# The RWKV-7 scan of a streaming encoder: the key turn split by heads and moved to another PSUM bank, key products with 128 stationary columns, and a new order on four engines

## The reference

```python
def step(s, inp):
    r_t, w_t, k_t, v_t, aa_t, bb_t = inp
    sa = jnp.einsum('bhij,bhj->bhi', s, aa_t)
    s = s * w_t[:, :, None, :] + sa[..., None] * bb_t[:, :, None, :] + v_t[..., None] * k_t[:, :, None, :]
    return s, jnp.einsum('bhij,bhj->bhi', s, r_t)

s_last, ys = lax.scan(step, s0.astype(f32),
                      (tm(r_h), tm(w_h), tm(k_h), tm(v_h), tm(-kk), tm(kk * a_h)))
mean = jnp.mean(y, axis=-1, keepdims=True)
var = jnp.mean(jnp.square(y - mean), axis=-1, keepdims=True)
```

## Time and profile before

| | |
|---|---|
| median of 3 runs | 3098.05 us (3096.76 to 3098.19) |
| the profiled execution's own time | 3098.73 us |
| its span | 3096.9 us |
| PE busy in the span | 2966.1 us, 96% |
| DVE, ACT, POOL busy | 57%, 33%, 30% |
| scan, about | 1650 to 2095 us of the span |

### The profile page before, as it was taken

The page is one execution under the profiler, slowest core; times in us unless marked ns, Lnnn a source line. Parts: engine busy times, 40 slices in busy tenths (PEclk is TensorE's granted clock), DMA queues, the critical chain, the costliest instruction groups (busy, mean ns, idle before and its releaser), DMA issues.

```text
span 3096.9 us, 63576 instructions
## 1 busy us (share of the span) xinstructions
PE 2966.1 (96%) x27602; PEld 2870.8 (93%) x27602; DVE 1755.0 (57%) x1813; ACT 1022.1 (33%) x1281; POOL 939.2 (30%) x525
## 2 busy tenths in 40 slices
PE   8999999999999999879998999998999999999998
PEld 7899999999999998879997878888999999999997
DVE  7765766555556567612114666663565555656557
ACT  6533411111111112543325778773311111111113
POOL 1322232322222224313223555542232222222231
PEclk9999999999999999999999999998999999999999
DMA  3111111111111111052232223222111111111112
GB/s 109 46 45 41 36 49 42 42 48 42 48 42 48 42 43 34 23 228 85 91 109 89 74 76 88 74 58 87 42 42 48 42 48 42 48 42 42 48 42 72
DMA packets 88671, 185.46 MB, mean 60 GB/s; under 512 B 29024, under 2 KB 53088, under 8 KB 88416
## 3 DMA queue, kind: packets, MB, share of 16 engines
q1 hardware_dynamic: 81504, 154.73, 16.3%
q10 hardware_dynamic: 6912, 26.84, 2.1%
HBM read 145.01 MB, written 36.53 MB: 59 GB/s over the span
## 4 chain that ended last, share of the span: by engine, by line
PE 81%; DVE 13%; ACT 4%; issue 1%; POOL 1%; DMA 0%; DVEq 0%; SPq 0%; ACTq 0%; POOLq 0%
PE PS L1293 65%; PE PS L1503 11%; DVE T L1815 3%; DVE X L1815 2%; DVE T L1830 2%; PE PS L1429 2%; ACT T L509 1%; ACT L509 1%; DVE HL L1825 1%; PE PS L1383 1%; DVE T L1825 1%; PE PS L1345 1%; DVE T L1820 1%; DVE T L1957 1%; DVE X L1825 1%
## 5 line engine op out<-in xcount | busy, mean ns | idle before, releaser
L1090 POOL TENSOR_TENSOR WL<-RAW,WH 128x1024 fp32r<-128x1024 f32 x204 | 494.9, 2426 | 1397.1 <-ACT WH L509 1393.5
L1293 PE MATMUL PS<-HH,WH 128*128 128x364 f32 x3456 | 772.2, 332 | 33.7 <-DVE HL L1815 13.1
L1293 PE MATMUL PS<-HH,WL 128*128 128x364 f32 x3456 | 768.1, 331 | 0.0
L1293 PE MATMUL PS<-HL,WH 128*128 128x364 f32 x3456 | 765.4, 330 | 0.0
L1293 PEld LDWEIGHTS PS<-HH,WH 128*128 128x128 f32 x3456 | 601.8, 189 | 42.5 <-issue 15.3
L1293 PEld LDWEIGHTS PS<-HH,WL 128*128 128x128 f32 x3456 | 606.7, 189 | 0.0
L1293 PEld LDWEIGHTS PS<-HL,WH 128*128 128x128 f32 x3456 | 603.7, 189 | 0.0
L509 ACT ACTIVATE WH<-RAW 128x1024 fp32r<-128x1024 f32 x204 | 216.6, 1062 | 826.5 <-PE PS L1293 810.3
L1815 DVE TENSOR_TENSOR T<-PS,T 128x1092 f32<-128x1092 f32 x110 | 142.5, 1296 | 551.8 <-PE PS L1293 535.4
L1815 DVE TENSOR_TENSOR X<-PS,X 128x1092 f32<-128x1092 f32 (+2 forms) x240 | 292.8, 1220 | 235.0 <-PE PS L1293 216.6
L1293 PE MATMUL PS<-PH,WH 128*128 128x364 f32 x1248 | 278.4, 331 | 10.1 <-DVE X L1815 5.2
(11 more groups left out here) (186 smaller groups left out, 3252.3 us busy)
## 6 DMA issues: line engine op xcount, KB each, us to landing
RAW<-weights SPq DMA_DIRECT2D x204, 512.0 KB, 3.6
scratch<-T ACTq DMA_DIRECT2D x31, 546.0 KB, 3.0
scratch<-SR ACTq DMA_DIRECT2D x14, 546.0 KB, 2.9
X<-xT SPq DMA_DIRECT2D x8, 546.0 KB, 7.8
T<-scratch_m SPq DMA_DIRECT2D x8, 512.0 KB, 3.8
KK<-scratch SPq DMA_DIRECT2D x16, 192.0 KB, 2.9
LW<-scratch SPq DMA_DIRECT2D x16, 192.0 KB, 2.6
AA<-scratch SPq DMA_DIRECT2D x16, 192.0 KB, 3.3
```

Source lines behind the costliest of these rows:

```text
L1090: pool.tensor_tensor(out, full, hi, ALU.subtract).then_inc(*t.made(event))
L1293: mm = pe.matmul(acc[:, j, :], a, b[:, j * CW:(j + 1) * CW], start=(i == 0 and q == 0), stop=(i == len(blocks) - 1 and q == 2))
```

## The change

It has three parts, all within the scan.

1. `products`: for each chunk and head the two matmuls with 64 stationary columns (taken key, grown key) become one with 128 stationary columns. It gives the same numbers at the same place. A chunk takes 2 matmuls where it took 4, and they have the form 64 rows by 128 columns.
2. `key_turn` is called once for each head, and writes bank 7, which `spread` and `value_turn` use, in place of banks 3 and 4. `keys` on ACT follows by heads. `lower` need no longer wait for `keys`; `spread` does.
3. The lists of calls of PE, ACT and DVE are in a new order. POOL's is not changed; SP's wait only counts anew.

The diff, cut to its core:

```diff
@@ -994,12 +994,11 @@
                         act.wait_ge(*t.at("k_gln", job))
                         run(q1, q1, ACT.Exp, "k_grs", scale=-0.5, own=False)
-                def keys():
+                def keys(h):
                     if has_p:
-                        act.wait_ge(*t.next("k_tb", 2))
-                        run(G[:, pa:pz, :, 2 * CHUNK:].rearrange("p n h c -> p h n c"),
-                            PS[:, 3:5, 0:(pz - pa) * CHUNK].rearrange("p h (n c) -> p h n c", c=CHUNK), ACT.Copy, "k_bkt", own=False)
+                        act.wait_ge(*t.next("k_tb"))
+                        run(G[:, pa:pz, h, 2 * CHUNK:], bank(7, pz - pa), ACT.Copy, "k_bkt", own=False)
                 def outputs_y():
...
@@ -1009,36 +1008,37 @@
                         act.wait_ge(*t.next("k_y", 2))
                         run(Y[:, a:z, :], bank(1, z - a), ACT.Copy, "k_ys", own=False)
-                scaled_key()
                 turned_removal()
-                key_square()
                 key_factor()
-                turned(1)
-                decay_in()
                 centred_square()
                 if job == JOBS:
                     w_hi(W_OUT, M_OUT)
                     rows_in(0)
+                turned(1)
+                scaled_key()
                 solved_values()
+                decay_in()
                 solved_keys()
                 growth()
+                turned(2)
                 last_spill()
                 group_ln()
-                turned(2)
+                key_square()
+                values()
                 turned(3)
                 norm_ln()
                 group_exp()
                 if job == JOBS:
                     rows_in(1)
                 turned(4)
-                values()
+                norm_exp()
+                keys(0)
                 affine()
                 if job == JOBS:
                     rows_in(2, 3)
                 turned(5)
-                keys()
+                keys(1)
                 outputs_y()
-                norm_exp()
                 spread_out()
             for job in range(-3, JOBS + 1):
                 interval(job)
...
@@ -1657,38 +1657,39 @@
                     else:
                         held(("k_gm", 2 * q + 1))
                     for i in range(ga, gz):
-                        for s in range(2):
-                            for h in range(HEADS):
-                                mul(tile(3 + h, (h + s) % 2, i - ga, P), BK[HALF[h], i, s if h == 0 else 2 - s, :],
-                                    AR[HALF[h], i, :, :].rearrange("p s c -> p (s c)"), "k_g" if i == gz - 1 else None)
+                        for h in range(HEADS):
+                            mul(PS[:, 3 + h, (i - ga) * P:(i - ga + 1) * P], BK[HALF[h], i, h:h + 2, :].rearrange("p s c -> p (s c)"),
+                                AR[HALF[h], i, :, :].rearrange("p s c -> p (s c)"), "k_g" if i == gz - 1 else None)
                 def value_turn():
                     if not has_p:
                         return
                     pe.wait_ge(*t.next(f"dma_in{pb}", 10 if pb == NB - 1 else 5))
-                    held(("k_rae", max(inv, 0)))
+                    held(("k_rae", inv) if inv > 0 else ("k_bkt", 2 * q))
                     for i in range(pa, pz):
                         for h in range(HEADS):
                             mul(tile(7, 1 - h, i - pa), VV[HALF[h], i * CHUNK:(i + 1) * CHUNK], IST[HALF[h], :],
                                 "k_tv" if i == pz - 1 else None)
-                def key_turn():
+                def key_turn(h):
                     if not has_p:
                         return
-                    held(("k_gm", 2 * q + 2))
+                    if h == 0:
+                        held(("k_bk", q + 1), ("k_bkh", q + 1), ("k_bk1", q + 1), ("k_vt", 2 * q + 2))
+                    else:
+                        held(("k_bkt", 2 * q + 1))
                     for i in range(pa, pz):
-                        for h in range(HEADS):
-                            mm = pe.transpose(PS[:, 3 + h, (i - pa) * CHUNK:(i - pa + 1) * CHUNK],
-                                              BK[HALF[h], i, h:h + 2, :].rearrange("p s c -> p (s c)"), IST[HALF[h], :])
-                            if i == pz - 1:
-                                mm.then_inc(*t.made("k_tb"))
+                        mm = pe.transpose(PS[:, 7, (i - pa) * CHUNK:(i - pa + 1) * CHUNK],
+                                          BK[HALF[h], i, h:h + 2, :].rearrange("p s c -> p (s c)"), IST[HALF[h], :])
+                        if i == pz - 1:
+                            mm.then_inc(*t.made("k_tb"))
                 def lower_begin():
                     if has_p:
-                        held(("k_bkt", q + 1), ("k_eye", 1))
+                        held(("k_gm", 2 * q + 2), ("k_eye", 1))
                 def lower(i):
...
@@ -1700,7 +1701,7 @@
                 def spread_begin():
                     if has_l:
-                        held(("k_rae", inv), ("k_vt", 2 * min(q, JOBS - 1) + 2))
+                        held(("k_rae", inv), ("k_vt", 2 * inv + 2), ("k_bkt", 2 * min(q, JOBS - 1) + 2))
                 def spread(i):
...
@@ -1765,34 +1772,35 @@
                 turned_alone(0)
                 forward_0_and_solve()
                 value_turn()
-                forward_1_and_variances()
+                variances_and_forward_1()
                 fresh_out()
                 turned_1_and_moves()
                 fresh_state()
+                forward_alone(2)
+                link_state(0)
                 key_squares()
-                forward_alone(2)
                 turned_alone(2)
-                link_state(0)
+                link_out(0)
+                link_state(1)
                 products(0)
-                link_out(0)
                 forward_alone(3)
                 turned_alone(3)
-                link_state(1)
                 link_out(1)
+                link_state(2)
+                link_out(2)
+                key_turn(0)
                 products(1)
-                link_state(2)
+                link_state(3)
                 forward_4_and_bonus_sums()
-                link_out(2)
                 turned_alone(4)
-                link_state(3)
                 link_out(3)
-                key_turn()
                 link_state(4)
+                key_turn(1)
                 link_out(4)
-                turned_alone(5)
+                link_state(5)
                 link_out(5)
-                link_state(5)
-                lowers_and_spreading()
+                turned_5_and_lowers()
+                spread_alone()
             for job in range(-3, JOBS + 1):
                 interval(job)
...
@@ -2285,29 +2293,29 @@
                             ALU.mult, ALU.add, "k_cent", own=False)
                 near()
+                centred()
                 scan()
-                centred()
                 mask(1)
+                key()
+                removal()
                 mask(2)
-                removal()
-                key()
                 grown_half()
                 transfer()
                 reading()
+                state(0)
+                mask(3)
                 floor()
-                mask(3)
-                state(0)
                 weighted()
+                state(1)
                 masked(0)
                 mask(4)
-                state(1)
                 state(2)
+                state(3)
                 masked(1)
-                state(3)
                 mask(5)
                 state(4)
+                state(5)
                 bonus()
-                state(5)
                 inverse()
             for job in range(-3, JOBS - 1):
```

More of the change, by code:

```diff
@@ L445, in interval @@
                     f, b = divmod(job + 4, NB)
-                    sp.wait_ge(*t.at("k_g", 8 * (job + 2)))
+                    sp.wait_ge(*t.at("k_g", 4 * (job + 2)))
                     sp.wait_ge(*t.at("k_bonus", job + 2))
@@ L1718, in forward_0_and_solve, with variances_and_forward_1 @@
                         solve(i)
-                def forward_1_and_variances():
+                def variances_and_forward_1():
                     forward_begin(1)
@@ L1742, in forward_4_and_bonus_sums, with turned_5_and_lowers @@
                         forward(4, i)
-                def lowers_and_spreading():
+                def turned_5_and_lowers():
+                    turned_begin(5)
                     lower_begin()
-                    spread_begin()
                     for i in range(6):
+                        turned(5, i)
                         lower(i)
-                        spread(i)
                 def forward_alone(k):
@@ L1756, in forward_alone, with spread_alone @@
                         forward(k, i)
+                def spread_alone():
+                    spread_begin()
+                    for i in range(6):
+                        spread(i)
                 def turned_alone(k):
@@ L2247, in masked @@
```

(2 more changed lines are left out.)

## The result

The changed kernel takes 3110.09 us (median of 8 runs, 3105.32 to 3111.51) against 3098.12 us (8 runs, 3096.76 to 3105.24) for the kernel before: ratio 1.0033, with a 95% interval of 1.0023 to 1.0043. It is slower, as forecast, but by 12 us (10 by the ratio) where the prediction had 27. The profiled execution took 3106.04 us.

What follows compares the result with a forecast made beforehand. PE was taken to set the pace. +8 us from forms, transposes and gains plus 19 us for the wait at `key_squares` made +27, to 3125 us; own range 3112 to 3134, full range 3103 to 3141.

Steps and rivals of the forecast that it cites:

- The stop: PE waits at `key_squares` for ACT's square, delayed behind `turned(2)` and the table load: 0.95 us, 20 intervals, 19 us.
- 0.62 + 0.35 - 0.60 = +0.37 us, times 22 = +8: Per interval in the scan: changes of matmul form 0.62, one-head transposes 0.35, less gains of new orders 0.60; +8 us.
- Costs charged in full: On PE, two more visits to another matmul form, 0.62 us, and serial transposes of one head, 0.35, per interval.
- (c): PE's waits for SS and before the products get more slack: a gain of 0.2 us an interval.
- (a): `turned(0)` on PE waits less for DVE's FIRST, as lower products end before the spreading: gain taken as 0.35 us.
- (b): `solve` on PE waits less for ACT's RA, as the scaled key moves back: gain taken as 0.15 us.
- Products, zero: 128-column products on PE keep the streaming pace, two steps of 0.11 us a chunk as before: zero change.
- The bound at the bottom: For the products: if PE were paced by records, 24 fewer would save 0.67 us an interval.
- Transposes of one head: In the key turn, six transposes of each half run serially, 6 + 6 steps instead of 6: 0.35 us more.
- Paced by records: Rival: a floor of 0.028 us per PE record, not streaming, sets the pace; faster, 3090 us; chance 0.09.
- the stop is hidden: Rival: PE reaches `key_squares` late anyway, so the 19 us shrink; 3104 us or less; chance 0.11.
- twice the stop: Rival: late square also delays later work, or 128-column loads aren't hidden: another 0.6 us an interval, 3138 us; chance 0.15.

Runs made afterwards that it cites:

- The change without the stop: Changed kernel with the group norm's Ln and its table load back ahead of `turned(2)` on ACT: 3092.00 us, ratio 0.9983 to the kernel before.
- The tail: End of PE's interval (`turned(5)` beside lower products, then spreading): undone in changed kernel, ratios 1.0033 and 1.0044; done alone in kernel before, 1.0013.

## Why the prediction was right about the sign, and wrong about the size

**The stop.** Forecast 19 us: 20 times 0.95. Measured 17.6 us in 20 waits, 0.88 each (15.0 in 17 in the second profile), and 15.5 us of time when it is taken away alone. Mechanism, place and number of times were right, and the size nearly. In its working one reading is off: 0.85 us for `fresh_state` is the time of 24 records, and the interval of the earlier trace rows has 20, which take 0.12 less. The Trainium skill ("ScalarE: Activation LUTs", section "What ACT_TABLE_LOAD costs") gives a switch of tables 1.28 us for the load and 1.38 more for a drain. Here the load takes 1.28 us, starts 0.01 us after the instruction ahead of it has ended, and Q starts 0.02 us after its end, so there is no drain to be seen. With one the stop would have been over 2 us, by an estimate from that page's figure.

**What failed** is the sum of the rest, "0.62 + 0.35 - 0.60 = +0.37 us, times 22 = +8". The change without the stop measures -5 us (-8 to -2.5). Two things in it were wrong:

- *Costs charged in full, 0.62 + 0.35 = 0.97 an interval, 21 us.* The prices themselves were about right: a gap of 0.15 us ahead of each block in another form and 0.15 to 0.20 behind it, streaming at the old pace, six transposes of one half as long as twelve of both, and +0.89 in the shortest sums of the three blocks. But the mean of these sums rose by only 0.38 an interval (0.36 in the kernel without the stop), some 8 us. The prediction added the new gaps to blocks in which PE stood and waited already: the second products took 0.80 us in quarters, and 0.80 in the wide form with both its gaps. It had 0.2 an interval, 4 us, for such waits, in its gain (c). Costs less (c) were thus to be 17 us, and 8 were seen.
- *Gains (a) and (b) of the new orders, 0.4 an interval, 9 us.* What is left for them is -5 - 8 = -13 us. FIRST gave nothing (0.87 us from the means to `turned(0)` before and after). RA gave what was forecast: from `turned(0)` to `forward(0)` the mean went from 0.96 to 0.80 us. The rest, some 10 us, is only what the subtraction leaves. The tail is worth nothing in this kernel, so it is to be looked for in the new order of the links and masks, but no experiment took these moves apart, and the cause stays open.

The first error is about 9 us and the second about 4, both to the slow side, and together they are the distance from +8 to -5. Trace sums of one profile carry about 0.1 us an interval and a ratio 3 us, so the split is no finer than that. Adding the stop's 15.5 back to -5 gives the measured +10 of itself, as the 15.5 is the difference of the two ratios; it checks nothing.

What the experiments on single terms say of the rest:

- *Products, zero*: the pace of the streaming was right (39.2 us for half the records). With its visit the wide form is 2 us slower than quarters in the changed kernel and 3 without the stop. The traces have +0.20 us at the first group, some 5 us, and nothing at the second. In the order of before it is free. The bound at the bottom, 0.67 an interval for a pace by records, is refuted by the same row.
- *Transposes of one head*: 2 us and 0.18 us in the trace with both heads in a row, where the second half overlaps the first. With the heads apart, as in the change, the full step.

**Rivals.** "Paced by records" is refuted by the pace of `AR,BK`; "the stop is hidden" by the 20 waits and by the 15.5 us; "twice the stop" by the 15.5 us and by the longest of these waits, 1.2 us. The 3110 us lie just below the forecast's own range, 3112 to 3134. They lie within 3103 to 3141 only through the room left for the rival of the hidden stop, whose mechanism did not hold: that part was luck.

**What stays open**: besides the 10 us above, how much wide products take away from the "issue" stops. In the order of before "issue" fell by 7.0 us. In the changed kernel without the stop wide products had 9.9 us of it and quarters 7.6 in the same row, and two profiles of the changed kernel had 3.8 and 8.7. One profile each can't settle it.

## What to carry to other kernels

When an in-order engine's list is reordered, look for the long instruction that was hidden in a wait (here a 1.28 us table load ahead of `turned(2)`): moved behind the instruction that waits, it is paid in full, and taking just that one move back turned a slower kernel into a faster one. Before a new gap is added to the sum, look whether the engine already waits at that place: here the wide products' gaps cost nothing in the second group, where PE waited before, and 0.2 us in the first. And measure a serial block where it will stand: six transposes of one half cost the full 0.36 us alone, and 0.18 when the other half followed at once. A forecast of many small terms needs each one measured alone, since here two errors of 9 and 4 us had the same sign.

## What the runs showed of the hardware

PE's stops put down to "issue" name no other engine that PE waited for. In the trace of the kernel before they follow packets on the instruction queue, whose row in the view of the DMA queues for the steady stretch is (packets, MB, share):

```profile
q8 instruction: 90, 1.47, 1.6%
```

That is one packet of 16 KB every 4.2 us. Of the packets that start at 1844.52, 1848.65 and 1853.31 each is followed 2.3 to 2.5 us later by the end of a stop of PE; the first two are these:

```profile
1846.94 0.45 PE L1503 MATMUL PS<-B,MT 64*64 64x64 f32 x9 [1.37 <-issue]
...
1851.16 0.33 PE L1503 MATMUL PS<-AR,BK 64*64 64x128 f32 x2 [0.40 <-issue]
```

Elsewhere a packet has no stop behind it. My reading, argued and not shown, is that PE at this density of small instructions (11163 records in 380 us) sometimes runs out of instructions before the next block has come. The time in these stops differs between two executions of the same kernel, 3.8 and 8.7 us in this stretch of the changed one, so a difference of that size between two kernels says nothing. No experiment here changed the fetch alone.
